# A hybrid decoder step on one core: two more raw weight buffers for fourteen units, a score step moved inside a chunk, and the samples' products in lumps

## The reference, cut to what matters

```python
h = x + W_out[ window_attention(n1) ; gated_groupnorm(retention(n1)) ]   # n1 = RMSNorm(x), one W_in for all heads
h = h + cross_attention(RMSNorm(h), mem_k, mem_v)    # 4 heads, 256 memory tokens; the prompt's come from w_xk, w_xv
h = h + W_down relu(RMSNorm(h) W_up)^2
y = RMSNorm_final(h)                                 # also returned: last keys and values, retention states
```

## Time and profile before

| | us |
|---|---|
| median of 3 runs | 1548.38 |
| lowest, highest | 1547.46, 1548.71 |
| the profiled execution's own time | 1549.24 |
| its span, first to last instruction | 1547.1 |
| TensorE busy | 1518.4 (98%) |
| VectorE busy | 655.3 (42%) |
| ScalarE busy | 448.0 (29%) |
| GpSimd busy | 230.2 (15%) |

### The profile page before, as it was taken

The page is one execution under the profiler, slowest core; times in us unless marked ns, Lnnn a source line. Parts: engine busy times, 40 slices in busy tenths (PEclk is TensorE's granted clock), DMA queues, the critical chain, the costliest instruction groups (busy, mean ns, idle before and its releaser), DMA issues.

```text
span 1547.1 us, 24477 instructions
## 1 busy us (share of the span) xinstructions
PE 1518.4 (98%) x9798; PEld 1446.0 (93%) x9798; DVE 655.3 (42%) x1233; ACT 448.0 (29%) x834; POOL 230.2 (15%) x233
## 2 busy tenths in 40 slices
PE   7999999999899999999999999999999999999998
PEld 7999888888799988878999999999999999999998
DVE  5543766455754533453374322333223432234222
ACT  6422444332411222332243310232102321133213
POOL 1200000134455300034450000000000000000144
PEclk9999999989899999999999999999999999999999
DMA  6564010111231201064531111111111111111102
GB/s 218 195 187 110 29 41 28 42 45 55 87 114 52 96 27 30 26 225 156 190 96 55 41 49 46 42 50 46 42 54 42 41 55 42 54 42 41 55 28 113
DMA packets 153554, 115.50 MB, mean 75 GB/s; under 512 B 13680, under 2 KB 142896, under 8 KB 153200
## 3 DMA queue, kind: packets, MB, share of 16 engines
q1 hardware_dynamic: 142736, 79.11, 17.2%
q0 software_dynamic: 8544, 31.04, 5.9%
q10 hardware_dynamic: 2192, 4.20, 0.8%
HBM read 101.19 MB, written 14.16 MB: 75 GB/s over the span
## 4 chain that ended last, share of the span: by engine, by line
PE 92%; DVE 3%; DMA 2%; issue 1%; ACT 1%; POOL 0%; SPq 0%; POOLq 0%; ACTq 0%; DVEq 0%
PE ps L337 27%; PE ps L338 26%; PE ps L339 26%; PE ps L1214 4%; PE ps L1635 2%; PE ps L1653 2%; PE ps L1304 1%; PE ps L1328 1%; DVE wlo L322 1%; ACT whi L317 1%; DMA raw<-in_w_xv 1%; DVE state L2127 1%; DMA raw<-in_w_in 1%; PE ps L1425 1%; PE ps L1423 1%
## 5 line engine op out<-in xcount | busy, mean ns | idle before, releaser
L337 PE MATMUL ps<-xhi,whi 128*128 128x352 f32 x1392 | 460.5, 331 | 11.1 <-issue 6.2
L338 PE MATMUL ps<-xlo,whi 128*128 128x352 f32 x1392 | 449.7, 323 | 0.0
L339 PE MATMUL ps<-xhi,wlo 128*128 128x352 f32 x1392 | 449.6, 323 | 0.0
L337 PE MATMUL ps<-yhi,whi 128*128 128x352 f32 x1136 | 371.7, 327 | 0.6 <-DVE wlo L322 0.6
L339 PE MATMUL ps<-yhi,wlo 128*128 128x352 f32 x1136 | 364.4, 321 | 0.0
L338 PE MATMUL ps<-ylo,whi 128*128 128x352 f32 x1136 | 364.3, 321 | 0.0
L337 PEld LDWEIGHTS ps<-xhi,whi 128*128 128x128 f32 x1392 | 264.2, 190 | 21.5 <-issue 14.3
L338 PEld LDWEIGHTS ps<-xlo,whi 128*128 128x128 f32 x1392 | 264.6, 190 | 0.1
L339 PEld LDWEIGHTS ps<-xhi,wlo 128*128 128x128 f32 x1392 | 263.8, 190 | 0.0
L317 ACT ACTIVATE whi<-raw 128x1024 fp32r<-128x1024 f32 x130 | 137.1, 1055 | 383.4 <-PE ps L339 334.3
L337 PEld LDWEIGHTS ps<-yhi,whi 128*128 128x128 f32 x1136 | 213.1, 188 | 4.4 <-DVE wlo L322 2.1
(11 more groups left out here) (271 smaller groups left out, 1332.1 us busy)
## 6 DMA issues: line engine op xcount, KB each, us to landing
raw<-in_w_up SPq DMA_DIRECT2D x32, 512.0 KB
raw<-in_w_down SPq DMA_DIRECT2D x32, 512.0 KB
raw<-in_w_xo SPq DMA_DIRECT2D x16, 512.0 KB
kx<-in_cache_mem_k POOLq DMA_DIRECT2D x16, 512.0 KB, 5.6
raw<-in_w_in SPq DMA_DIRECT2D x14, 512.0 KB
spill<-hT POOLq DMA_DIRECT2D x8, 528.0 KB, 6.8
xin<-in_x_prompt SPq DMA_DIRECT2D x8, 512.0 KB, 7.6
raw<-in_w_xk SPq DMA_DIRECT2D x8, 512.0 KB
```

The costliest lines, as they stand in the source:

```text
L337: pe.matmul(out, whi[:, q, k, :], x1, start=k == 0, stop=False)
L338: pe.matmul(out, whi[:, q, k, :], x2, start=False, stop=False)
L339: mm = pe.matmul(out, wlo[:, q, k, :], x1, start=False, stop=k == KB - 1)
```

## The change

Three things are changed.

First, a tile `raw2` of two raw buffers is placed where the memory rows stood. Units 6 to 19 use it in every second pair (6, 7, 10, 11, 14, 15, 18, 19), so that these units have four raw buffers in turn. The loads of units 8 to 21 wait for the low half of the unit four before; those of 6 and 7 wait as before. SP waits for the turned memory rows ahead of unit 6.

Second, in sliding tile n = 0 the first scores of tile 1 move from the place ahead of chunk 1 to its middle.

Third, the samples' products that stood in quarters or eighths between blocks are issued whole: scores and values ahead of block 4 of the gate chunk, the retention output after the chunk and `ret_turn_out(5)`, the state sums after `out_product(1, 1)`. `ret_turn_out(7)` moves from the middle of `out_product(1, 0)` to the place ahead of it. On VectorE, n = 7 gets the order of the other n (update inside the statistics, evacuation of the gate after `normed`), and the split of `U_OUT + 1` moves behind it; the samples' low halves move behind `out_evacuate(1, 1)`.

The diff, cut to its core:

```diff
         memx, _ = place("memx", [P, 2, D], at=at_y + 2 * BLK)
+        raw2, _ = place("raw2", [P, 2, KB, P], at=at_y + 2 * BLK)
...
+        s_raw2 = [S("raw2_loaded_even"), S("raw2_loaded_odd")]
+        RAW2 = range(6, U_IN + 4)
+
+        def second(u):
+
+            return isinstance(u, int) and u in RAW2 and u // 2 % 2 == 1
+
+        def raw_of(u, q):
+            return raw2[:, q] if second(u) else raw[:, q]
+
+        def raw_ready(u, q):
+            if second(u):
+                return s_raw2[q], LOAD * ((u - RAW2[0]) // 4 + 1)
+            before = len([v for v in RAW2 if v % 2 == q and second(v) and not (isinstance(u, int) and v > u)])
+            return s_raw[q], LOAD // 2 * (u - q) + LOAD - LOAD * before
+
+        def raw_read(u):
+
+            return u - 3 if isinstance(u, int) and u in range(RAW2[0] + 2, RAW2[-1] + 3) else u - 1
...
-            wait(sp, s_wlo, u - 1)
+            wait(sp, s_wlo, raw_read(u))
...
+                sp.dma_start(dst, src).then_inc(raw_ready(u, q)[0], LOAD - 16 * n if last else 16)
...
-            act.wait_ge(s_raw[q], LOAD // 2 * (u - q) + LOAD)
+            act.wait_ge(*raw_ready(u, q))
...
-            act.activation(whi[:, q], raw[:, q], ACT.Copy).then_inc(s_whi, 1)
+            act.activation(whi[:, q], raw_of(u, q), ACT.Copy).then_inc(s_whi, 1)
...
-            dve.tensor_tensor(wlo[:, q], raw[:, q], whi[:, q].bitcast(F32), ALU.subtract).then_inc(s_wlo, 1)
+            dve.tensor_tensor(wlo[:, q], raw_of(u, q), whi[:, q].bitcast(F32), ALU.subtract).then_inc(s_wlo, 1)
...
             for u in range(2, U_RET):
+                if u == RAW2[0]:
+                    sp.wait_ge(s_xT, XT + 1)
                 first_unit(u)
...
                 win_turn_p(n, 0)
-                if n < NQ - 1:
+                if 0 < n < NQ - 1:
                     win_scores(n + 1, 0)
-                product(pe, u, q, 1, xhi, xlo, CW)
+                product(pe, u, q, 1, xhi, xlo, CW, halfway=(lambda: win_scores(1, 0)) if n == 0 else None)
...
-            def sample_scores(k):
-
-                kv, b0 = (k - KB // 2) // 2, (k % 2) * NB // 2
-                r = slice(kv * HD, (kv + 1) * HD)
-                for b in range(b0, b0 + NB // 2):
-                    pe.matmul(ps[:, 2 + kv, b * 16:b * 16 + 16].rearrange("p (g t) -> p g t", t=DT), kcT[r, b, :], smz[r, 0:G, b * DT:b * DT + DT], start=True, stop=True)
-                if k % 2 == 1:
+            def sample_scores():
+                for kv in range(NKV):
+                    r = slice(kv * HD, (kv + 1) * HD)
+                    for b in range(NB):
+                        pe.matmul(ps[:, 2 + kv, b * 16:b * 16 + 16].rearrange("p (g t) -> p g t", t=DT), kcT[r, b, :], smz[r, 0:G, b * DT:b * DT + DT], start=True, stop=True)
+                for kv in range(NKV):
+                    r = slice(kv * HD, (kv + 1) * HD)
                     mm = pe.matmul(ps[0:TS, 2 + kv, P:2 * P].rearrange("p (b g t) -> p b g t", g=G, t=DT), smz[r, 4, :],
                                    smz[r, 0:G, :].rearrange("p g (b t) -> p b g t", t=DT), start=True, stop=True)
-                    if kv == NKV - 1:
-                        mm.then_inc(S("smp_scores"), 1)
+                mm.then_inc(S("smp_scores"), 1)
...
-            def sample_values(k):
...
+            def sample_values():
...
-                for b in range(b0, b0 + NB // 2):
-                    mm = pe.matmul(ps[r, 2, b * 16:(b + 1) * 16], vc[:, b, r], psT[:, kv * P + b * 16:kv * P + (b + 1) * 16],
-                                   start=False, stop=b == NB - 1, skip_group_check=True)
-                if k == KB - 1:
-                    mm.then_inc(S("smp_out"), 1)
+                    for b in range(NB):
+                        mm = pe.matmul(ps[r, 2, b * 16:(b + 1) * 16], vc[:, b, r], psT[:, kv * P + b * 16:kv * P + (b + 1) * 16],
+                                       start=False, stop=b == NB - 1, skip_group_check=True)
+                mm.then_inc(S("smp_out"), 1)
...
-            def sample_ret_out(k):
...
+            def sample_ret_out():
...
-            def sample_state_sum(b):
-
...
-                pe.wait_ge(S("smp_kz_masked"), b + 1)
...
+            def sample_state_sum():
+                pe.wait_ge(S("smp_kz_masked"), NB)
+                for b in range(NB):
+                    for h in range(RH):
+                        r, s = slice((h % 2) * RQ, (h % 2 + 1) * RQ), b * 2 + h // 2
+                        mm = pe.matmul(ps[r, 2 + s // 4, (s % 4) * RV:(s % 4 + 1) * RV], kzm[:, b, h * RQ:(h + 1) * RQ], vrs[:, h * RV:(h + 1) * RV], start=True, stop=True)
+                mm.then_inc(S("smp_state_sum"), 1)
...
-                def sample_step(k):
-                    if k < KB // 2:
-                        return
-                    if k == KB // 2:
-                        banks_read(n)
-                        if n == 1:
-                            sample_turn_keys()
-                        if n == 3:
-                            sample_ret_turn()
-                        if n == 4:
-                            sample_ret_inner()
-                        if n == 6:
-                            sample_turn_out()
-                        if n == 7:
-                            sample_turn_normed()
+                def sample_step():
+                    banks_read(n)
+                    if n == 1:
+                        sample_turn_keys()
                     if n == 2:
-                        sample_scores(k)
+                        sample_scores()
+                    if n == 3:
+                        sample_ret_turn()
                     if n == 4:
-                        sample_values(k)
-                    if n == 5:
-                        sample_ret_out(k)
-
-                gate(FILL[n][0], sample_step)
-                if n < NQ - 1:
-                    ret_turn_out(n)
+                        sample_values()
+                        sample_ret_inner()
+                    if n == 6:
+                        sample_turn_out()
+                    if n == 7:
+                        sample_turn_normed()
+
+                gate(FILL[n][0], halfway=sample_step)
+                if n == NQ - 1:
+                    out_product(0, 0)
+                ret_turn_out(n)
                 if n == 2:
                     sample_turn_scores()
                 if n == 3:
                     sample_turn_probs()
+                if n == 5:
+                    sample_ret_out()
                 for i in FILL[n][1:]:
                     gate(i)
 
-            def last_turn(k):
-                if k == KB // 2:
-                    ret_turn_out(NQ - 1)
-
-            out_product(0, 0)
-            out_product(1, 0, last_turn)
+            out_product(1, 0)
             out_product(0, 1)
-            out_product(1, 1, sample_state_sum)
+            out_product(1, 1)
+            pe.wait_ge(s_ron, RH * NQ)
+            pe.wait_ge(s_rstate, RH * NQ)
+            pe.wait_ge(S("smp_affine"), 4)
+            pe.wait_ge(s_rf, RH * NQ)
+            sample_state_sum()
             out_product(0, 2)
             out_product(1, 2)
...
                 dve.wait_ge(s_ro, n + 1)
-                if n == NQ - 1:
-                    gate_evacuate(FILL[n][0])
-                stats(ret_o, gst, gmv, gvar, s_rvar, (lambda: ret_update(n)) if n < NQ - 1 else None)
+                stats(ret_o, gst, gmv, gvar, s_rvar, lambda: ret_update(n))
                 if n < NQ - 1:
                     ret_keys(n + 1)
-                if n in (0, 1, 3, 5, 7):
-                    u = {0: U_GATE + 1, 1: U_GATE + 2, 3: U_GATE + 3, 5: U_OUT, 7: U_OUT + 1}[n]
+                if n in (0, 1, 3, 5):
+                    u = {0: U_GATE + 1, 1: U_GATE + 2, 3: U_GATE + 3, 5: U_OUT}[n]
                     split_lo(dve, u, u % 2)
...
                 wait(dve, s_roT, n)
...
-                if n < NQ - 1:
-                    gate_evacuate(FILL[n][0])
+                gate_evacuate(FILL[n][0])
...
-            ret_update(NQ - 1)
+            split_lo(dve, U_OUT + 1, 1)
             dve.wait_ge(s_back[0], 64)
             out_evacuate(0, 0)
             mixed_lo(1)
...
             out_evacuate(0, 1)
             mixed_lo(2)
+            out_evacuate(1, 1)
             for i, m in ((0, 0), (4, 10)):
                 dve.wait_ge(S("smp_hi"), i // 4 + 1)
                 dve.tensor_tensor(xlo[:, i:i + 4, TP:T], smz[:, m:m + 4, :], xhi[:, i:i + 4, TP:T].bitcast(F32), ALU.subtract).then_inc(S("smp_lo"), 1)
-            out_evacuate(1, 1)
             dve.wait_ge(S("smp_state_sum"), 1)
```

More of the change, by code:

```diff
@@ L1366, in _, with gate @@
                     win_scores(n + 1, 1)
-            def gate(i, between=None):
+            def gate(i, halfway=None):
                 u, q, c = gate_unit(i)
                 pe.wait_ge(s_wlo, u + 1)
-                product(pe, u, q, c, xhi, xlo, CW, ready=between)
+                product(pe, u, q, c, xhi, xlo, CW, halfway=halfway)
             gate(0)
@@ L1521, in sample_ret_out @@
```

(19 more changed lines are left out.)

35 lines of the change are left out of this document (10 added, 25 removed).

## The result

The changed kernel takes 1532.57 us (six runs, 1528.93 to 1535.10) against 1547.92 us (six runs, 1546.49 to 1549.08): a ratio of 0.9901, with a 95% interval of 0.9886 to 0.9916. The profiled execution took 1535.10 us (span 1533.0), 14.1 us less than the one of before; it was the slowest of the six.

A forecast was written before the change was run, and what follows sets the result against it. TensorE, busy 98% of the span, was taken as the bound. The terms -3.7 - 1.2 - 3.4 + 0.5 - 1.0 + 3.4 + 0.3 - 2.5 = -7.6 us, off the median of 1548.38, gave 1540.8 us; range 1536 to 1546.5.

The forecast's parts named there:

- Memory rows: Keys' and values' memory units: four raw buffers let loads start earlier, so late units vanish; gain 3.7 us, 2.5 to 3.9.
- rival (c): Four buffers gain only the values' half, as unit 7 lands late, and the tail comes 0.8 later: 1542.7 us; chance 0.12.
- First tile: First sliding tile: TensorE's 1.37 us wait for the bias adds goes, one break costs 0.20; gain 1.2 us, 0.9 to 1.4.
- Output lump: Samples' retention output: four breaks of 0.20 us saved, +0.5 waiting for normed(5), -1.0 of clock (between -5.1 and +1.0).
- Values and sums: Samples' values and state sums: three and seven breaks of 0.20 us saved, one short low-clock stretch for both, +3.4 us.
- Scores: Samples' scores: three breaks of 0.20 us saved, the same low-clock stretch kept, 0, between -3.4 and +1.7 us.
- The tail: Before out_product(0, 1): mixed_lo(1) starts 0.3 us later, the 5.43 us pause splits into two of about 3, low clock gone, -2.5.
- rival (a): The clock holds in the values' and sums' lumps: 3.4 us less, 1537.4 us; chance 0.20.
- (b): The clock falls for a short time in both the values' and sums' lumps: 3.4 us more, 1544.2 us; chance 0.20.
- (d): Slower: every lump brings a low-clock stretch of 10.2 us, +12.0, 1552.8 us; chance 0.06.
- (e): Small products in lumps wait as long as at a break, none of 17 saved: +3.4, 1544.2 us; chance 0.05.

The follow-up runs named there:

- arrive_2: The changed kernel with GpSimd's gating of the third column waiting for the second of VectorE's eight subtractions of mixed_lo(1): 1533.65 us.
- the order's own run: The kernel before with only the n = 7 order on TensorE and VectorE changed, sample products still broken up: 1543.35 us, ratio 0.9973.
- pool_waits: The kernel before with one added wait holding GpSimd's last four gating products until the eight subtractions of mixed_lo(1) are done: 1543.83 us, ratio 0.9974.

## Why the prediction was wrong

**Memory rows: right.** Forecast -3.7, measured -3.3. The values' units are dense and ScalarE no longer waits for w_xv. Of the keys' 1.1 us 0.5 stayed (0.2 to 0.5 in nine executions): rival (c), by which all of it stays, fell. Unit 7 came 0.2 us late, not more, though two loads follow its own at once. With that the trace is in keeping with the rule quoted there (the Trainium skill, DMA: Bandwidth & Descriptors, Two DMAs through the same engine are not ordered), that descriptors in one queue start in order but are pipelined; it tests no more of it. The earlier trace rows came from an execution that lost somewhat more than the mean one.

**First tile: right.** -1.2 forecast, -1.45 measured.

**Output lump: right in sum.** TensorE stood 0.17 us for `normed(5)`, not 0.5. The low-clock stretch was 6.8 us long in place of 10.2, and the whole lost 1.4 (1.8 on the mean of nine executions with the lump and ten without), against 1.3 forecast (-0.8 + 0.5 - 1.0).

**Values and sums: 1.4 us too dear, for the price of a break.** One short stretch for the two was forecast, 3.4 us of price against 0.6 and 1.4 of breaks: +1.4. The price of the clock was right in sum: the changed kernel had a stretch 3.4 us long in each place, which cost 1.5 and 1.6 (against 25.2 and 11.5 us where the clock held). But the breaks gave more, and the two came to +0.7 and -0.7. The sums' seven breaks gave 2.3, some 0.33 each, and the values' three 0.85 with the clock at 1.00 on both sides (26.06 us in pieces; with the lump, in `arrive_2`):

```profile
339.19:364.40 25.21, 24.88 (x204) 22.41 (x202) 14.10 (x50) 8.78 (x19) 10.28 (x14) 1.00 0.30 85
```

The forecast's 0.20 counted the two turns between dense and small products alone. The small ones, too, follow each other slower in pieces: eight of the sums take 0.58 us (427.82 to 428.40), in the lump 0.46 (64 in 3.70). The first row is of the kernel before, the others of the changed kernel:

```profile
428.40 0.43 PE L337 MATMUL ps<-xhi,whi 128*128 128x352 f32 x1
...
417.37 3.77 PE L1558 MATMUL ps<-vrs,kzm 32*64 32x128 f32 x64
421.07 0.66 PE L357 MATMUL ps<-xhi,whi 128*128 128x352 f32 x1
```

**Scores: the step that failed most.** The term was -0.6 of breaks and 0 for the clock ("I take the same low stretch"). Measured -3.0, and -4.4 between the means of nine executions with the lump and eight with four pieces. The row at 0.70 was read as a stretch that small products bring, which the run without them bears out. What was missed is that its length changes with how far they are spread: in four pieces it was 10.2 or 13.7 us long in all eight executions, in a lump 0 to 6.8 us in all nine. The bound of -3.4 stood in the prediction and was not used.

**The tail: the second.** The start of `mixed_lo(1)` was sized well: 7.24 us after `out_product(0, 0)` begins, against 7.17 before (+0.07, forecast +0.3). Its duration was taken over from the earlier trace rows as if it belonged to the instructions. It was that of a contest with GpSimd, and in the new order VectorE wins it: the end comes 2.9 us earlier. Of the two pauses of about 3 us that were forecast the one ahead of `out_product(1, 0)` was 2.2 us long (1.3 and 0.9), and the one ahead of `out_product(0, 1)` did not come. The gain of 2.5 for the low clock came out as put (the chunk took 3.9 us in place of 6.58); in the changed kernel's profiled execution a stretch of 3.4 us fell into `out_product(1, 0)` and took 1.4 back. -4.2 instead of -2.2; -5.4 in the order's own run, where no such stretch came. The prediction did look at this port, with the Trainium skill (SBUF — State Buffer, Who interferes with whom), but only for a new meeting, never for the old one dissolving. The same section adds that the order of issue decides who blocks. The traces don't bear that out one instruction at a time: in both kernels GpSimd's product started some 0.01 us ahead of a subtraction (414.26 and 414.27 us; 404.90 and 404.91), and it got in in the first and not in the second.

**The range.** Scores and output had an end 3.4 and 4.1 us below the value taken, and the low end of 1536.0 added up neither; it only reached past rival (a). The tail's own end lay 0.3 below: the subtractions' free duration was not in it. No rival had the failed terms either. With -3.0 for the scores, -4.2 for the tail and 0 for values and sums the sum would have been 1540.8 - 2.4 - 2.0 - 1.4 = 1535.0 us, still 2.4 above the median: the rows come from the slowest of the six runs, and 0.7 of its gain is in none of the terms.

**Rivals.** Of five profiled executions with both new lumps the clock fell in both places in three, as in (b), in the values alone in one, and in neither in one, as in (a); the price of either was hidden under the failed terms. (d) did not come: the longest low stretch in a new lump was 6.8 us. (e) fell: the sums lost 2.3 us where seven breaks were priced at 1.4.

**Open.** What lets GpSimd in with the old order. All eight profiled executions with it and no wait show the subtractions in step with GpSimd, all eight with the update moved and GpSimd inside their run show them free, whenever it arrived (0.42 to 1.99 us in). Readiness of their inputs doesn't explain it: ScalarE had written the last of the high halves before the run began in either order (411.57 against 413.40 before, 402.59 against 404.48 after). Open too is why the low-clock stretches change in length from one execution to the next, and why the scores keep the clock better in a lump and the values in pieces.

## What to carry to other kernels

A duration read from a stretch where two engines contend isn't a property of the instruction: before a chain is re-timed, price it at the free duration too, because a move upstream may dissolve the meeting. Small products can cost TensorE's clock, and whether pieces or a lump cost more has to be tried for each group: on the mean the lump made the scores' stretch 4.4 us shorter and the values' 1.1 us longer. Price both forms from rows at both levels of the clock, and price a break by the whole period of a piece, not by its turns alone. Where several terms have a far end on the same side, let the range add some of them.

## What the runs showed of the hardware

A run of VectorE subtractions of two SBUF operands, 0.43 us apart, drew out a GpSimd product of 0.9 us to 3.88 us, until the run was over; in another order of the same instructions the two took turns at 1.1 us. A wait on GpSimd that looks like a loss (`pool_waits`) gained 4.6 us.

The stretches of the mixer in which TensorE was granted 1.2 GHz were 3.4, 6.8, 10.2 or 13.7 us long, and a second execution of the same program had them at four of five places, with other lengths. At the scores' lump the stretch from gate to gate took 17.02 us without one, 18.56 with 3.4 us of it and 20.09 with 6.8.
